# Scores of two attentions on row tiles, negated queries, and sixteen adaLN chunks moved between projections

## The chip, the cores and the metric

The kernel runs on one core of a Trainium2 chip, as one program. The metric is the device time of one execution in microseconds (us). A core has TensorE (PE, matrix products, weight loads shown apart as PEld), VectorE (DVE), ScalarE (ACT), GpSimd (POOL), and SyncE (SP), which here only issues DMAs. Each engine has its own instruction queue; they wait for each other by semaphores.

## The reference

One inference step of a trunk with two layers, on 128 context tokens (group i) and 512 latent tokens (group ii, an 8 x 64 grid) of width 1024, in float32. Each layer, cut to what matters:

```python
shift1, scale1, gate1, shift2, scale2, gate2 = split(silu(c) @ w_ada + b_ada, 6)   # per group
h = rmsnorm(x) * (1 + scale1) + shift1
u_hy, u_na, u_da, u_gate = split(h @ w_in)
y_hy = hyena(u_hy)                      # short conv, two long convolutions by DFT
# NA: 8 heads of 64. context: plain softmax attention over context;
# latent: 8 rows x 16 columns around the query with a relative bias, and 128 cached context keys
s = q @ k.T * 64**-0.5 + bias           # outside the neighbourhood: -1e30
y_na = softmax(s) @ v
# DA: 8 heads, two maps of 32. latent: all 512 latent keys (rotated) and 128 cached keys
p1, p2 = softmax(q1 @ k1.T * 32**-0.5), softmax(q2 @ k2.T * 32**-0.5)
y_da = rmsnorm((p1 - lam * p2) @ v) * subln * (1 - lam_init)
x = x + gate1 * ((sigmoid(u_gate) * lifts of the three y, summed) @ w_out)
x = x + gate2 * swiglu_ffn(rmsnorm(x) * (1 + scale2) + shift2)
```

Outputs are both groups' final rmsnorm and the context keys and values of both attentions.

## The kernel before

Activations stay in SBUF with channels on partitions; the 640 tokens (128 context, 512 latent) are the free dimension. All weights come as 292 strips of 128 x 1024 f32 (512 KB), in a fixed order written out by hand: per layer 12 strips for Hyena (`S_UHY`), 12 for NA (`S_NA`: 4 for queries, 4 for keys, 4 for values), 12 for DA, 36 for gates and lifts, 8 for the output projection and 66 for the FFN. A product is made exact enough by splitting both sides in a rounded high part and a rest, and by three products (`tiles_of`, L446, 48 matmuls a strip; `v_strips`, L467, for values). SP loads a strip (three buffers), POOL writes its high part `whi` (L428) and its low part `wlo` (L430), PE waits for `w_split`. `w_used` rises when PE starts a strip and lets POOL overwrite the high part of the strip before last.

The adaLN modulation of a layer is 48 chunks of 128 outputs; `ada_dot` (L1179) makes one on DVE as two dot products of 128 x 1024 (context and latent), from a 512 KB chunk that ACT's queue loads with `ada_load` (L866), which waits until a buffer is used. In layer 0, chunks 0 to 23 are made at the start, chunks 24 to 39 (`N_ADA1` to `N_ADA2`, 16 chunks, four buffers) between the short convolutions of the Hyena strips (DVE list at L1309 to L1314, ACT's PSUM copies at L974 to L979), the rest in the FFN. ACT waits for the second modulation (`s_modr`) before it loads the first spectrum.

After the Hyena outputs (`s_yhy`), ACT issues loads of the cached NA keys, values and the bias table `rpbr` (L1017 to L1019), then copies the NA projections out of PSUM (L1023). DVE expands the bias table to `bexp` (L1370).

NA runs 40 times (5 query blocks of 128 x 8 heads). Block 0 is the context with 128 keys; blocks 1 and 4 have 3 key blocks, blocks 2 and 3 have 4. Channels hold two heads of 64 per 128 partitions, so DVE masks the queries of a pair to each head's rows (`na_queries`, L1414) and PE multiplies with all 128 rows. Per head: scores, a mask product from bf16 (L645 to L648), on DVE bias and maximum in one (L1388) and its negation `nmx` (L1392), on ACT the exponential with its sum (L1038), on PE the turn of the probabilities (L658), a copy on DVE (L1400), on PE the product with values (L674). PE's list is: scores of head n+1, turn of n, values of n-1.

DA also runs 40 times, with four 32-row groups in 128 partitions (two heads, two maps). DVE masks the queries (`da_queries`, L1464). The two maps use three PSUM banks, with the keys of the two maps in different order:

```python
for n in range(40):
    if n + 2 < 40:
        da_scores(n + 2, True)     # both maps' cache keys, map 1's 512 latent keys
    da_turn(n)
    if n + 2 < 40:
        da_scores(n + 2, False)    # map 2's 512 latent keys
    da_pv(n)
```

DVE reduces each map for its maximum (L1473), negates and scales both (L1475), later forms p1 - lam' p2 in two pieces because of the key order (L1488, L1489); ACT makes both exponentials (L1071, L1073) and copies the turned probabilities `dpt` (L1084); PE turns (L735, L739) and multiplies (L748).

## Time and profile before

| | |
|---|---|
| median of 3 runs | 3244.84 us (3239.64 to 3246.84) |
| the profiled execution | 3243.62 us |
| its span, first to last instruction | 3241.8 us |
| PE busy | 2960.7 us, 91% |
| DVE, ACT, POOL busy | 1506.6, 584.4, 1563.9 us |
| mean granted TensorE clock | 0.946 |

The span is what the profile covers; what lies around it is 1.8 us. A row of a group of instructions has line, engine, operation, tiles as out<-in, shapes and count, then busy time, mean ns of one, and the idle time of its engine just before with the instruction that ended it. PE's records overlap, since matmuls are pipelined: start to start is the time that one costs. An f32 matmul is two records.

### The profile page before, as it was taken

The page shows a single profiled execution, that of the slowest core. Times are in us where ns is not written, and L with a number is a line of the kernel's source. Part 1 is how long each engine was busy: PE and PEld are TensorE (multiplying, and loading weights), DVE is VectorE, ACT ScalarE, POOL GpSimd, SP SyncE. Part 2 cuts the span into 40 slices and gives each one's busy share as a digit, 9 for nine tenths or more (in the row PEclk, how much of TensorE's full clock was granted, in tenths as well). Part 3 has the DMA queues.
Part 4 walks back from the last instruction along what each step waited for, and adds up shares of the span by engine and source line. Part 5 has one row for each costly group of instructions (what it writes and reads, how often), then busy time and mean ns, then how long its engine had stood idle before and what let it go on. Part 6 is the DMA issues. An engine that isn't in the chain of part 4 may idle for free.

```text
span 3241.8 us, 42762 instructions
## 1 busy us (share of the span) xinstructions
PE 2960.7 (91%) x17564; PEld 2614.0 (81%) x17564; DVE 1506.6 (46%) x2553; ACT 584.4 (18%) x1189; POOL 1563.9 (48%) x588
## 2 busy tenths in 40 slices
PE   5898689998979998999998989998979998999997
PEld 1447659895569997999997959896569997999997
DVE  6885871645742214448653572655741124420113
ACT  1123110314520002000102111313520002100100
POOL 1003407061027765778775707061027765777764
PEclk8899799998979998999998999998989998999998
DMA  4434323020002222335432223020002222322222
GB/s 176 136 120 160 91 80 98 4 75 17 1 28 77 75 70 92 110 112 174 147 108 87 72 78 95 11 69 23 1 27 72 79 67 96 99 72 72 79 69 75
DMA packets 76790, 258.86 MB, mean 80 GB/s; under 512 B 9107, under 2 KB 12691, under 8 KB 75060
## 3 DMA queue, kind: packets, MB, share of 16 engines
q1 hardware_dynamic: 49148, 176.96, 17.3%
q10 hardware_dynamic: 27448, 79.17, 7.1%
q8 instruction: 139, 2.28, 0.3%
q14 instruction: 55, 0.45, 0.0%
HBM read 237.75 MB, written 18.35 MB: 79 GB/s over the span
## 4 chain that ended last, share of the span: by engine, by line
PE 77%; DVE 14%; ACT 3%; issue 2%; DMA 2%; DVEq 1%; ACTq 1%; POOLq 0%; POOL 0%
PE PS L446 57%; PE PS L467 3%; PE PS L726 3%; DVE adap L1179 3%; PE PS L530 2%; PE PS L748 2%; PE PS L674 1%; PE PS L735 1%; PE PS L645 1%; PE PS L500 1%; PE PS L613 1%; DVE mx L1473 1%; PE PS L658 1%; PE PS L720 1%; DVE yt L1334 1%
## 5 line engine op out<-in xcount | busy, mean ns | idle before, releaser
L428 POOL TENSOR_SCALAR whi<-wraw 128x1024 fp32r<-128x1024 f32 x292 | 838.2, 2870 | 1606.3 <-PE PS L446 1538.6
L446 PE MATMUL PS<-hhi,whi 128*128 128x320 f32 x3072 | 717.9, 315 | 66.6 <-DVE hlo L1163 43.3
L430 POOL TENSOR_TENSOR wlo<-wraw,whi 128x1024 fp32r<-128x1024 f32 x292 | 725.6, 2485 | 43.0
L446 PE MATMUL PS<-hlo,whi 128*128 128x320 f32 x3072 | 710.5, 313 | 0.0
L446 PE MATMUL PS<-hhi,wlo 128*128 128x320 f32 x3072 | 710.2, 313 | 0.0
L446 PEld LDWEIGHTS PS<-hhi,whi 128*128 128x128 f32 x3072 | 522.2, 192 | 80.9 <-issue 32.5
L446 PEld LDWEIGHTS PS<-hlo,whi 128*128 128x128 f32 x3072 | 523.9, 192 | 0.0
L446 PEld LDWEIGHTS PS<-hhi,wlo 128*128 128x128 f32 x3072 | 523.1, 191 | 0.0
L1179 DVE CUSTOM_DVE_ANT_0 adap<-ada,cond 128x1024 f32<-128x1024 f32 x192 | 338.7, 1764 | 35.0 <-DMA ada<-in_w_ada 12.8
L1562 DVE SCALAR_TENSOR_TENSOR x<-PS,mod,x 128x128 f32<-128x128 f32 x144 | 54.5, 433 | 300.0 <-PE PS L446 300.0
L1595 DVE TENSOR_TENSOR gact<-silu,PS 128x640 f32<-128x640 f32 x44 | 36.1, 821 | 334.8 <-ACT silu L1129 334.8
L446 PE MATMUL PS<-ahi,whi 128*128 128x320 f32 x704 | 163.4, 314 | 13.1 <-DVE alo L1598 13.1
L1473 DVE TENSOR_REDUCE mx<-PS 128x1 f32<-128x640 f32 (+1 forms) x160 | 112.8, 713 | 107.5 <-PE PS L720 53.7
L446 PE MATMUL PS<-alo,whi 128*128 128x320 f32 x704 | 162.6, 313 | 0.0
L446 PE MATMUL PS<-ahi,wlo 128*128 128x320 f32 x704 | 162.4, 312 | 0.0
L1129 ACT ACTIVATE silu<-PS 128x640 f32<-128x640 f32 x44 | 31.1, 706 | 677.0 <-PE PS L446 677.0
L1547 DVE TENSOR_TENSOR sig<-sig,PS 128x640 f32<-128x640 f32 x32 | 26.3, 822 | 271.2 <-PE PS L446 271.2
L726 PE MATMUL PS<-dak,dqz 128*128 128x512 f32 x256 | 134.1, 606 | 0.0
L446 PEld LDWEIGHTS PS<-ahi,whi 128*128 128x128 f32 x704 | 120.0, 191 | 14.2 <-DVE alo L1598 14.2
L748 PEld LDWEIGHTS PS<-dav,dpt 128*128 128x128 f32 x544 | 72.2, 203 | 61.6 <-ACT dpt L1084 60.7
L446 PEld LDWEIGHTS PS<-ahi,wlo 128*128 128x128 f32 x704 | 120.0, 191 | 0.0
L446 PEld LDWEIGHTS PS<-alo,whi 128*128 128x128 f32 x704 | 120.0, 191 | 0.0
(233 smaller groups left out, 4044.8 us busy)
## 6 DMA issues: line engine op xcount, KB each, us to landing
wraw<-in_w_strips SPq DMA_DIRECT2D x292, 512.0 KB, 3.6
ada<-in_w_ada ACTq DMA_DIRECT2D x72, 512.0 KB, 4.5
ada<-in_w_ada SPq DMA_DIRECT2D x24, 512.0 KB, 3.9
spectra<-hst ACTq DMA_DIRECT2D x48, 256.0 KB, 2.0
hld<-spectra ACTq DMA_DIRECT2D x8, 768.0 KB, 5.1
hld<-spectra ACTq DMA_DIRECT2D x12, 512.0 KB, 3.6
cond<-conds ACTq DMA_DIRECT2D x3, 1024.0 KB, 4.8
x<-in_x_in SPq DMA_DIRECT2D x1, 2560.0 KB, 14.7
```

The lines of the kernel that those rows point to most:

```text
L428: nc.gpsimd.tensor_scalar(hi, raw, 1.0, None, ALU.mult)
L430: nc.gpsimd.tensor_tensor(lo, raw, hi, ALU.subtract).then_inc(w_split, 1)
L446: ins = pe.matmul(out[:, h, :], w[:, kt, :], mv[:, h * HALF:(h + 1) * HALF], start=start and m == 0, stop=stop and m == 2)
L467: ins = pe.matmul(PS[:, i, :], hp[:, k, i * 128:(i + 1) * 128], w, start=(k == 0 and m == 0), stop=(k == KD - 1 and m == 2))
L500: pe.matmul(PS[:, 4 + g % 3, :], farg[lay][:, i * 128:(i + 1) * 128], fw3[:, 2 * o + d, :], start=True, stop=True).then_inc(s_hmm, 1)
L530: ins = pe.matmul(out, w, heo[:, i, half, :], start=(r == 0), stop=(r == len(tiles) - 1))
L726: pe.matmul(PS[:, b + 2 * m, :], q[m], dak[:, ch, C:T], start=True, stop=True).then_inc(s_ds, 1)
L748: ins = pe.matmul(PS[:, 7, 128:192], dpt[n % 2][:, i, :], v, start=(r == 0), stop=(r == len(vs) - 1))
L1179: ins = V.tensor_tensor_reduce(adap[s][:, :], ada[s][j][:, :], cond[s][:, c, :], 1.0, 0.0, ALU.mult, ALU.add, mraw[:, 2 * m + c:2 * m + c ...
L1473: V.tensor_reduce(mx[:, q + m:q + m + 1], PSF[:, 512 * b + lo:512 * b + hi], AX, ALU.max)
L1562: ins = V.scalar_tensor_tensor(x[:, m, cols], src, mod[:, gate + m, sgm:sgm + 1], x[:, m, cols], ALU.mult, ALU.add)
L1595: V.tensor_tensor(halves(gact[j % 2][:, :]), halves(silu[j % 2][:, :]), pair(2 * (j % 2) + 1), ALU.mult).then_inc(s_gact, 1)
```

## The change

1. NA scores: `na_scores` now does a pair of heads. The query masking is gone: each head's product uses only its 64 rows of queries and keys. Mask products of both heads come first, then both latent products, then both cache products. Scores have four PSUM banks; turned probabilities and outputs moved to others.
2. The queries are negated (and scaled) when they leave PSUM, the mask and bias are negated, and DVE takes the minimum. That is the bias of the exponential at once (scale -1), so `nmx` and its operation are gone. DA queries are also scaled there.
3. DA scores: map m of a head uses its 32 rows. The latent keys of both maps now have the same order in PSUM (`DA_MAP = 896` columns apart), map 2 in two products of 384 and 128. One reduce covers both maps, one operation forms the difference. Cached keys come from the host with the four groups apart and zeros between (1 MB, was 256 KB), and are multiplied over all 128 rows, after the turn.
4. Layer 0's adaLN chunks 24 to 39 move to the NA projection: their loads stand in ACT's queue behind the NA cache loads and between its PSUM copies, with three buffers (was four); DVE makes them behind the bias expansion and before the first NA head.
5. In layer 0, for strips 13 to 23 (NA, `HI_ON_ACT`), ACT makes the high part, in its queue ahead of the copy of the strip before; POOL makes only the low part.

```diff
-ADA_SLOTS = (2, 4, 4)
+ADA_SLOTS = (2, 3, 4)
+HI_ON_ACT = range(S_NA + 1, S_NA + N_NA)
...
             for n in range(DEPTH * STRIPS):
-                pool.wait_ge(w_in[n % 3], 16 * (n // 3 + 1))
-                if n >= 2:
-                    pool.wait_ge(w_used, n)
-                nc.gpsimd.tensor_scalar(hi, raw, 1.0, None, ALU.mult)
-                pool.drain()
+                if n in HI_ON_ACT:
+                    pool.wait_ge(w_hi, n - HI_ON_ACT.start + 1)
+                else:
+                    pool.wait_ge(w_in[n % 3], 16 * (n // 3 + 1))
+                    if n >= 2:
+                        pool.wait_ge(w_used, n)
+                    nc.gpsimd.tensor_scalar(hi, raw, 1.0, None, ALU.mult)
+                    pool.drain()
                 nc.gpsimd.tensor_tensor(lo, raw, hi, ALU.subtract).then_inc(w_split, 1)
...
+                def na_scores(u):
+                    qb, ch = u // 4, u % 4
+                    heads = [(PS[:, (2 * u + i) % 4, :], slice(64 * i, 64 * i + 64)) for i in range(2)]
+                    if u >= 2:
+                        pe.wait_ge(s_np, nth(lay, s_np, 2 * u - 2))
+                    if qb:
...
+                        for out, r in heads:
+                            pe.matmul(out[:, lat], identb[:, :], maskb[:, MASK0[j]:MASK0[j] + nb, :],
+                                      start=True, stop=False)
+                        for out, r in heads:
+                            pe.matmul(out[:, lat], naq[r, ch, qb * 128:qb * 128 + 128],
+                                      nak[r, ch, C + b0 * 128:C + (b0 + nb) * 128], start=False, stop=True)
+                    for out, r in heads:
+                        pe.matmul(out[:, cache] if qb else out[:, 0:128], naq[r, ch, qb * 128:qb * 128 + 128],
+                                  nckT[r, ch, :] if qb else nak[r, ch, 0:C], start=True, stop=True).then_inc(s_ns, 1)
...
                 for n in range(40):
-                    if n + 1 < 40:
-                        na_scores(n + 1)
+                    if n % 2 == 0 and n + 2 < 40:
+                        na_scores(n // 2 + 1)
...
+                def da_scores(n):
+                    r1, r2 = (slice(64 * (h % 2) + 32 * m, 64 * (h % 2) + 32 * m + 32) for m in range(2))
+                    q1, q2 = (daq[r, ch, qb * 128:qb * 128 + 128] for r in (r1, r2))
...
+                    pe.matmul(PS[:, b, :], q1, dak[r1, ch, C:T], start=True, stop=True)
+                    pe.matmul(PS[:, b + 2, 0:384], q2, dak[r2, ch, C + 128:T], start=True, stop=True)
+                    pe.matmul(PS[:, b + 1, 384:512], q2, dak[r2, ch, C:C + 128], start=True, stop=True)
+                def da_cache_scores(n):
...
+                    k = dckb[:, h // 2, 256 * (h % 2):256 * (h % 2) + 256]
+                    pe.matmul(PS[:, b + 1, 0:128], q, k[:, 0:128], start=True, stop=True)
+                    pe.matmul(PS[:, b + 2, 384:512], q, k[:, 128:256], start=True, stop=True).then_inc(s_ds, 1)
...
                 for n in range(40):
                     if n + 2 < 40:
-                        da_scores(n + 2, True)
+                        da_scores(n + 2)
                     da_turn(n)
                     if n + 2 < 40:
-                        da_scores(n + 2, False)
+                        da_cache_scores(n + 2)
                     da_pv(n)
...
-                if lay == 0:
-                    act.dma_start(cond[1][:, :, :], conds).then_inc(s_cond[0], 16)
-                for k in range(ADA_SLOTS[1] if lay == 0 else 0):
-                    ada_load(1, k, (lay, N_ADA1 + k))
...
-                    if o == 0:
-                        act.wait_ge(s_modr, nth(lay, s_modr, 2))
...
                 act.dma_start(rpbr[:, :, :], a["rpb"][lay]).then_inc(s_ncache, 16)
+                if lay == 0:
+                    act.dma_start(cond[1][:, :, :], conds).then_inc(s_cond[0], 16)
+                    for k in range(ADA_SLOTS[1]):
+                        ada_load(1, k, (lay, N_ADA1 + k))
+                def strip_hi(n):
+                    if n in HI_ON_ACT:
+                        act.wait_ge(w_in[n % 3], 16 * (n // 3 + 1))
+                        act.wait_ge(w_used, n)
+                        A(whi[n % 2][:, :, :], wraw[n % 3][:, :, :], ACT.Copy).then_inc(w_hi, 1)
                 for n in range(8):
+                    strip_hi(lay * STRIPS + S_NA + n + 1)
                     act.wait_ge(s_nq, nth(lay, s_nq, n + 1))
-                    dst, sc = (naq, 0.125) if n < 4 else (nak, 1.0)
+                    dst, sc = (naq, -0.125) if n < 4 else (nak, 1.0)
                     A(halves(dst[:, n % 4, :]), pair((n + 3) % 4), ACT.Copy, scale=sc).then_inc(s_nqe, 1)
+                    for k in range(2 * n + 3, min(2 * n + 5, N_ADA2 - N_ADA1)):
+                        if lay == 0:
+                            ada_load(1, k, (lay, N_ADA1 + k))
...
+                for n in range(8, N_NA):
+                    strip_hi(lay * STRIPS + S_NA + n + 1)
...
-                    for k in range(2 * n, min(2 * n + 2, N_ADA2 - N_ADA1) if lay == 0 else 0):
-                        ada_dot(1, k, N_ADA1 + k)
...
+                if lay == 0:
+                    dve.wait_ge(s_cond[0], 16)
+                    for k in range(N_ADA2 - N_ADA1):
+                        ada_dot(1, k, N_ADA1 + k)
+                    modulation(lay, N_ADA1, N_ADA2)
+                    norm_scale(lay, 1)
...
                 def da_max(n):
...
-                        V.tensor_reduce(mx[:, q + m:q + m + 1], PSF[:, 512 * b + lo:512 * b + hi], AX, ALU.max)
-                    dve.drain()
-                    V.tensor_scalar(nmx[:, q:q + 2], mx[:, q:q + 2], -DA_SCALE, None, ALU.mult).then_inc(s_dm, 1)
...
+                    both = PSF[:, p0:p0 + 2 * DA_MAP].rearrange("p (m n) -> p m n", m=2)
+                    V.tensor_reduce(mx[:, q:q + 2], both[:, :, 0:keys], AX, ALU.min).then_inc(s_dm, 1)
```

The diff is cut: the old forms of the score functions and the two masking functions are left out, as are moved buffers and bank numbers.

## Rows read from the trace of the kernel before

**Rows 1.** Cores view: span and mean granted TensorE clock.
```profile
core 0: 3241.8 us, clock 0.946
```

**Rows 2.** Windows view: window, us, busy PE, PEld, DVE, ACT, POOL, granted clock, DMA share, GB/s.
```profile
281.30:388.90 107.60, 90.59 (x529) 88.53 (x528) 83.70 (x89) 10.02 (x56) 63.12 (x22) 0.87 0.48 158
388.90:483.60 94.70, 74.89 (x272) 49.05 (x272) 73.04 (x132) 14.66 (x31) 0.00 (x0) 0.89 0.20 67
483.60:569.90 86.30, 85.21 (x506) 78.83 (x504) 15.87 (x42) 8.11 (x13) 64.36 (x24) 1.00 0.30 95
745.90:919.10 173.20, 155.08 (x792) 100.13 (x792) 126.36 (x330) 83.99 (x200) 0.00 (x0) 0.92 0.00 1
1788.80:1866.50 77.70, 77.67 (x530) 77.40 (x528) 37.98 (x41) 10.57 (x55) 59.74 (x22) 1.00 0.24 75
1866.50:1949.10 82.60, 70.89 (x273) 46.52 (x273) 62.11 (x113) 13.71 (x26) 0.00 (x0) 0.98 0.23 77
```

**Rows 3.** Chain of waits, 290 to 400 us: start, us, what.
```profile
339.04 1.23 DVE adap L1179
340.39 3.23 DVE adap L1179
```

**Rows 4.** Timeline of PE, layer 0, Hyena strips; start, us.
```profile
334.92 0.90 PE L446 MATMUL PS<-hhi,whi 128*128 128x320 f32 x2 [4.36 <-ACT rawu L979]
```

**Rows 5.** Timeline of ACT in the same strips.
```profile
346.80 0.28 ACT L974 ACTIVATE rawu<-PS 128x128 f32<-128x128 f32 x1 [11.94 <-DVE mraw L1179]
```

**Rows 6.** Timeline of ACT after the Hyena outputs of layer 0.
```profile
494.94 0.34 ACTq L1017 DMA_DIRECT2D nckT<-in_cache_na_k  x1
...
496.36 0.71 ACT L1023 ACTIVATE naq<-PS 128x640 f32<-128x640 f32 x1 [2.38 <-issue]
```

**Rows 7.** Timeline of DVE, same place.
```profile
503.75 3.35 DVE L1370 COPY bexp<-rpbr 128x128 f32<-128x128 f32 x24 [6.70 <-DMA rpbr<-in_rpb]
```

**Rows 8.** DMA issues, 494 to 506 us: count, KB each, us to landing.
```profile
rpbr<-in_rpb ACTq DMA_DIRECT2D x1, 1060.0 KB, 7.9
```

**Rows 9.** DMA issues, 276 to 300 us.
```profile
cond<-conds ACTq DMA_DIRECT2D x1, 1024.0 KB, 9.7
```

**Rows 10.** Timeline of PE in one 4-block NA head.
```profile
618.22 0.86 PE L645 MATMUL PS<-nak,nqz 128*128 128x384 f32 x2
618.92 0.33 PE L647 MATMUL PS<-maskb,identb 128*128 128x384 bf16 x1
619.08 0.38 PE L648 MATMUL PS<-nckT,nqz 128*128 128x128 f32 x2
...
620.58 0.54 PE L645 MATMUL PS<-nak,nqz 128*128 128x384 f32 x1
```

**Rows 11.** Timeline of PE over one DA head and the next.
```profile
804.39 0.66 PE L720 MATMUL PS<-dckT,dqz 128*128 128x128 f32 x4
804.89 1.02 PE L726 MATMUL PS<-dak,dqz 128*128 128x512 f32 x2
805.90 0.66 PE L735 MATMUL PS<-ident,dp 128*128 128x128 f32 x4
...
806.50 1.02 PE L726 MATMUL PS<-dak,dqz 128*128 128x512 f32 x2
807.46 1.10 PE L748 MATMUL PS<-dav,dpt 128*128 128x64 f32 x8
...
808.63 0.66 PE L720 MATMUL PS<-dckT,dqz 128*128 128x128 f32 x4
...
810.74 0.66 PE L735 MATMUL PS<-ident,dp 128*128 128x128 f32 x4 [0.59 <-DVE dp L1489]
```

**Rows 12.** Timeline of ACT in the same DA head.
```profile
806.70 0.70 ACT L1084 ACTIVATE dpt<-PS 128x640 f32<-128x640 f32 x1 [0.61 <-PE PS L739]
```

**Rows 13.** Instruction groups in twenty DA heads: busy us, mean ns, idle before.
```profile
L1473 DVE TENSOR_REDUCE mx<-PS 128x1 f32<-128x640 f32 x40 | 32.8, 820 | 15.8 <-PE PS L726 15.8
...
L1488 DVE SCALAR_TENSOR_TENSOR dp<-dp,coef,dp 128x512 f32<-128x512 f32 x20 | 15.0, 752 | 1.5
```

174 lines of the change are left out of this document (63 added, 111 removed).

## The prediction

> **What bounds the kernel now.** The profile was read in this order: the span, busy time by stage, the chain of waits where two like stages differ, then the timelines of the two attention loops. The profiled execution spans 3241.8 us [rows 1]. The two layers run the same stages, so laying them side by side shows what layer 0 pays extra [rows 2]. From the end of the first Hyena strip to the end of the twelfth, layer 0 takes 107.6 us and layer 1 77.7 us; from there to the first strip of the NA projection, 94.7 and 82.6 us. The reader is to see DVE: 83.7 us busy in layer 0's strips and 38.0 us in layer 1's, while PE is 99.9% busy in layer 1 and 84% in layer 0, and its granted clock is 0.87 there against 1.00. The work that only layer 0 has there is 16 adaLN chunks of two dot products, each 1.23 us alone and 3.2 us where a POOL instruction is in the way [rows 3]. ACT stands in its queue at an adaLN load that waits for a dot (11.94 us), then empties PSUM late, and PE waits for that (4.36 us) [rows 4, 5]. So layer 0's Hyena part is bound by DVE through ACT's queue. The attention loops are different: PE has almost no idle time in them, and what sets a head's time is PE's own list (below).
>
> **The adaLN chunks leave the Hyena projection.** With 32 dots and the loads that block ACT gone, layer 0's stretch should become layer 1's: (107.6 + 94.7) - (77.7 + 82.6) = 42.0 us less. This holds the removed wait of the spectrum load for the second modulation, and the lower clock behind the stalls. Bounds: 30 us if only the strips gain (107.6 - 77.7 = 29.9), 42 if all. I take 42, since nothing else differs between the layers there.
>
> **They arrive in the NA projection.** That stretch has 86.3 us with only 15.9 us of DVE [rows 2], so 32 dots of 1.23 to 3.2 us (39 to 102 us; about 55 with one POOL conflict in four dots) fit in time. The order of ACT's queue does not fit. Strip 13's high part is now made by ACT, behind the wait for the Hyena outputs, three cache loads, the modulation vectors and three adaLN loads. The first cache load issues at 494.94 [rows 6], some 2 us earlier without POOL's strip in the way: 492.7. Three issues take 1.42 us up to the next instruction, seven 3.3 to 4.3 (the last ones move twice as much), so ACT copies from 497.0. A copy of 128x640 takes 0.71 us [rows 6], one of 128x1024 about 1.1 (estimate, 0.71 x 1.6), then POOL's low part about 2.6 us (64.4 / 24 is 2.7 for both kinds): strip 13 is ready at 500.7. Strip 12 begins at 483.6 and takes 7.06 (77.7 / 11), so PE would idle from 490.7, 10 us. Strip 14's copy stands behind the loads of chunks 3 and 4, which wait for dots 0 and 1. DVE can begin these when the rpb table has landed (7.9 us) and 24 copies of 3.35 us together are done, at about 505.5 [rows 7, 8]; the modulation vectors take 9.7 us from issue and are there by about then [rows 9]. Two chunks at 2.6 us end at 510.8, then copy 1.1, low part 2.6 to 3.3 with a conflict: strip 14 starts near 516, where strip 13 would have ended at 507.8 at full clock and about 510.5 after such a gap. For the price of a gap I take the Hyena strips of layer 0: a granted clock of 0.87 over 107.6 us is 28 us at 1.2 in place of 2.4 GHz, and with some five gaps each has 5.6 us of that and loses 2.8 us of work. From strip 15 on, the loads are two strips ahead, POOL has half its work per strip, and PE sets the pace. Sum: 10 + 5 idle and 2 x 2.8 at half clock, about +20 us. Bounds: 12 (both idle times short, no half clock) to 42 (all strips paced as in layer 0's Hyena part, 107.6 / 11 = 9.8 us against 7.06 for 8 strips, on top of the start). The later strips' copies on ACT cost nothing: ACT is busy 8.1 of 86.3 us. If that cover went, PE would wait for a strip. The 1 MB of separated keys is loaded ahead of the twelve strips of the DA projection (12 x 7.06 us) and is hidden by them.
>
> **NA scores on row tiles.** A 4-block head takes 2.36 us (618.22 to 620.58), PE without a gap: latent scores 0.70, mask 0.16, cache scores 0.22, the rest 1.28 [rows 10]. Each f32 matmul is two records, so a head pair has four of about 0.35 and four of about 0.11. Two heads now lie on different 64 rows. If neighbours in the list on different rows run at the same time, the second half of head 0 covers the first of head 1, and the second of head 1 the first cache half: 0.35 x 3 + 0.11 x 3 = 1.4 in place of 1.84, 0.22 us a head. For 3-block heads the same working gives 0.17 (estimate, by the shorter moving side). So 16 x 0.22 + 16 x 0.17 = 6.2 us a layer, 12.5 us in both. If they do not overlap it is nothing, since the negation and the query masking leave DVE, which is not the bound there.
>
> **DA scores on row tiles.** Now a head takes 4.24 us, the next 4.84 (every second head DVE also masks the next queries, and PE waits 0.59): 4.54 on average [rows 11]. PE's list is: cache scores 0.50, first map 1.01, from the transposes to the PV product 1.56, PV 1.17. Afterwards the piece of 1.56 stays, because it is set by ACT's copy of the turned probabilities (806.70 + 0.70, PV at 807.46) [rows 11, 12], although the second map's 0.96 us is taken from under it and only the cache scores' 0.50 is put there. PV stays 1.17. All latent scores now stand together behind PV: two halves of 0.50, two of 0.375, two of 0.125, which is 2.0 us one after the other and 1.62 if the second half of the first map covers the first half of the second. A head: 1.56 + 1.17 + 1.62 = 4.35 us overlapped, 4.70 serial. DVE must fit under this. Its reduce of 640 takes 0.82 us and waited for PE [rows 13]; one over both maps about 1.5 (between 0.82 and 1.64), the joined sum at most 0.94 (0.75 x 640 / 512), small steps and output 0.8: about 3.3 us of work, and the chain transposes 0.65, cache 0.66, reduce 1.5, small steps and sum 1.4 is 4.2. So (4.54 - 4.35) x 32 x 2 = -12.2 us overlapped, (4.70 - 4.54) x 64 = +10 serial. I take overlap, as the tiles touch different rows and PSUM banks, but no row of before shows it.
>
> **Block 0.** Its 8 heads per stage lose the same masking and negation, in short chains that DVE is part of. The nearest row is the 0.59 us that masking cost a pair [rows 11]: 0.3 x 8 heads x 4 stages = -9.6 us. Bounds 0 and double that.
>
> **Going between full and row tiles.** It happens 2 x 20 pairs x 2 layers + 2 x 40 heads x 2 layers = 240 times. Below: nothing, as the change from f32 to bf16 and back around the mask leaves no gap. Above: the tail that a matmul has after its successor has started, 0.66 - 0.50 = 0.16 us [rows 11], 38 us in all. I take nothing. On this the Trainium skill speaks against the change: "TensorEngine Tiling (Array Packing)", Key Properties, says that changing the tiling mode drains the TensorE; by that the time would be up to the 38 us later. No row here has such a switch. "TensorE: Matmul & The Clock Gate", Part 3, says that tiles of different rows run concurrently while matmuls keep their order; by that the overlapped figures hold.
>
> **Sum.** -42 + 20 - 12.5 - 12.2 - 9.6 = -56 us. The profiled execution took 3243.6 us, so 3187; the median of the runs shown is 1.2 us above it: 3188 us.
>
> **Rivals.**
> The tiles run one after the other. For it: f32 halves of one tile share its rows, and the order is kept. Against: different rows. -42 + 20 + 10 - 9.6 = -22, 3223 us.
> Each switch drains. For it: the tail of 0.16 us exists. Against: dense lists show no gap today. -56 + 38 = -18, 3227 us.
> The chunks throttle the NA projection as they did the Hyena one. For it: the same loads in ACT's queue, three buffers. Against: DVE has no conv there. +42 in place of +20, 3210 us.
> Slower: the clock falls to half in the DA loop, because PE's idle moments (1.56 - 0.60 - 0.11 - 0.50, some 0.35 us a head) or the narrow tiles don't hold it up. At half clock PE's list of 4.0 us doubles, so a head takes about 8 us in place of 4.54. It decides from 16 of 64 heads (16 x 3.5 = 56 us); all would cost over 200 us, 3400 us. For it: the stage's clock is 0.92 already. Against: PE is 90% busy there and stays so [rows 2].
> The change does nothing measurable: that the moved dots cost as much as they cost before, with serial tiles.
>
> **Numbers.** Forecast 0.50; serial 0.14; drains 0.12; throttled projection 0.08; better than 3165 0.04; nothing 0.04; half clock or another loss 0.08. The range 3162 to 3228 holds the first four and ends where full drains do. Within 0.2% (6.5 us) is what a measurement of this kernel can't tell from no change: faster 0.88, same 0.04, slower 0.08.
>
> **What would show it.** Right: layer 0's Hyena strips at 7.05 us each; ACT's copy for strip 13 near 497 us less the 42 gained, PE idle some 10 and 5 us before strips 13 and 14 and none later; in DA a head every 4.3 to 4.4 us with the reduce over 1280 elements near 1.5 us; in NA 4-block heads at 2.1 us; in both, PE starts on different rows closer than one record's time. Wrong: heads at 4.7 us and more, gaps at each switch, a clock under 0.9 in either loop, or strips 15 to 20 spaced over 8 us.

## The result and the profile after

The changed kernel takes 3303.52 us (median of 4 runs, 3302.38 to 3306.26) against 3243.12 us for the kernel before in the same comparison: ratio 1.0187, 95% interval 1.017 to 1.0205. It is slower by about 60 us, where 3188 us, some 56 us less than before, was predicted.

The page of the kernel after: busy time of TensorE, and the granted clock in 40 slices.

```profile
PE 3058.2 (93%) x17692; PEld 2739.6 (83%) x17692; DVE 1416.3 (43%) x2169; ACT 594.6 (18%) x1200; POOL 1531.2 (46%) x577
...
PEclk9899989985569998999998999995559998999999
```

PE is busy for 93% of the span, more than the 91% before, and two groups of slices at 5 stand out. They are the differential attention (DA) of the two layers. The mean granted clock has gone from 0.946 to 0.891.

The windows view of the kernel after: first the Hyena stage from the end of strip 0 to the first strip of the neighborhood (NA) projection, that projection, and the NA attention, all of layer 0, then most of the DA attention of layers 0 and 1.

```profile
279.54:438.88 159.34, 149.60 (x802) 124.97 (x801) 100.47 (x154) 24.81 (x87) 59.37 (x22) 0.98 0.27 88
438.88:544.75 105.87, 88.99 (x506) 82.95 (x504) 61.99 (x106) 19.41 (x24) 37.81 (x13) 0.92 0.48 167
544.75:622.79 78.04, 71.88 (x556) 59.48 (x557) 47.26 (x126) 33.93 (x90) 0.00 (x0) 0.91 0.01 5
711.00:925.00 214.00, 208.84 (x822) 167.58 (x815) 99.13 (x191) 80.47 (x194) 0.00 (x0) 0.51 0.00 1
2217.00:2433.00 216.00, 211.73 (x818) 170.19 (x818) 99.16 (x193) 80.99 (x195) 0.00 (x0) 0.50 0.00 1
```

Set beside the kernel before, stage by stage. The NA attention is counted from the last value matmul of its projection to the next projection, the DA attention from its last value matmul to the first turn of its outputs:

| stage | before | after | difference | predicted |
|---|---|---|---|---|
| Hyena stage, layer 0 | 202.3 [rows 2] | 159.3 | -43.0 | -42 |
| NA projection, layer 0 | 86.3 [rows 2] | 105.9 | +19.6 | +20 |
| NA attention, layers 0 and 1 | 87.5 + 87.3 | 78.0 + 78.0 | -18.8 | -12.5 and half of -9.6 |
| DA attention, layers 0 and 1 | 189.9 + 188.6 | 241.6 + 243.6 | +106.7 | -12.2 and half of -9.6 |

The four sum to +64.5 us. The spans differ by 3300.6 - 3241.8 = 58.8; the other 6 us fell away in stretches the change does not touch, none over 2.6 us. So one stage makes the whole result. In it PE is busy 98% of the time, at a granted clock of 0.51 and 0.50, which is the lower level, 1.2 GHz. Before, it stood at half clock only through block 0 and in its last 9 us, and had 0.92 over all [rows 2].

PE's timeline of the kernel after, over one head of the DA loop of layer 0 and the start of the next, at half clock.

```profile
861.37 1.22 PE L720 MATMUL PS<-dak,daq 32*128 32x512 f32 x1
861.38 1.64 PE L721 MATMUL PS<-dak,daq 32*128 32x384 f32 x2
862.39 1.06 PE L720 MATMUL PS<-dak,daq 32*128 32x512 f32 x1
862.82 0.63 PE L722 MATMUL PS<-dak,daq 32*128 32x128 f32 x2
863.38 1.11 PE L741 MATMUL PS<-ident,dp 128*128 128x128 f32 x4
864.29 0.42 PE L745 MATMUL PS<-ident,dp 128*128 128x128 f32 x1
864.50 0.63 PE L731 MATMUL PS<-dckb,daq 128*128 128x128 f32 x2
864.93 0.63 PE L732 MATMUL PS<-dckb,daq 128*128 128x128 f32 x2
865.50 1.97 PE L754 MATMUL PS<-dav,dpt 128*128 128x64 f32 x8
...
867.83 1.22 PE L720 MATMUL PS<-dak,daq 32*128 32x512 f32 x1
```

A head takes 867.83 - 861.37 = 6.46 us, where two took 4.24 and 4.84 before [rows 11]. The tiles do overlap: L720 and L721 start 0.01 us apart, on 32 rows each (the "32x512"), and all latent scores are done in 863.38 - 861.37 = 2.01 us at half clock. There is no gap between the parts, so this is PE's list and nothing else, with each instruction taking twice its time. The clock was at full in layer 0's loop once, from 834.9 to 838.3 us.

PE's timeline of the kernel after, the one head whose scores ran at full clock. From 838.3 us on it is half again.

```profile
836.20 0.69 PE L720 MATMUL PS<-dak,daq 32*128 32x512 f32 x1
836.20 0.91 PE L721 MATMUL PS<-dak,daq 32*128 32x384 f32 x2
836.73 0.59 PE L720 MATMUL PS<-dak,daq 32*128 32x512 f32 x1
836.95 0.38 PE L722 MATMUL PS<-dak,daq 32*128 32x128 f32 x2
837.91 0.78 PE L741 MATMUL PS<-ident,dp 128*128 128x128 f32 x4 [0.57 <-DVE dp L1480]
```

The same scores take 1.13 us to their last end here (836.20 to 837.33), and PE then waits 0.57 us for VectorE's joined sum. So with the clock up the tiles overlap as the prediction meant them to.

### The profile page after: what moved, and what is told of

The parts are those of the page before. It is cut to its first block, busy times and chain, and to the rows that moved or that the text cites. A ratio compares the mean times of both kernels' runs of the same rounds, so it can differ in the third digit from the quotient of the medians.

```text
span 3300.6 us, 42311 instructions
## 1 busy us (share of the span) xinstructions
PE 3058.2 (93%) x17692; PEld 2739.6 (83%) x17692; DVE 1416.3 (43%) x2169; ACT 594.6 (18%) x1200; POOL 1531.2 (46%) x577
## 4 chain that ended last, share of the span: by engine, by line
PE 85%; DVE 9%; ACT 3%; DMA 1%; issue 1%; DVEq 1%; ACTq 1%; POOL 0%
PE PS L445 58%; PE PS L754 5%; PE PS L466 3%; PE PS L529 2%; PE PS L720 2%; PE PS L741 2%; PE PS L673 2%; PE PS L721 1%; PE PS L657 1%; DVE adap L1195 1%; PE PS L499 1%; DMA ada<-in_w_ada 1%; PE PS L596 1%; PE PS L732 1%; PE PS L731 1%
## 5 line engine op out<-in xcount | busy, mean ns | idle before, releaser
L427 POOL TENSOR_SCALAR whi<-wraw 128x1024 fp32r<-128x1024 f32 x281 | 800.4, 2848 | 1555.1 <-PE PS L445 1498.4
L429 POOL TENSOR_TENSOR wlo<-wraw,whi 128x1024 fp32r<-128x1024 f32 x292 | 730.7, 2502 | 186.5 <-ACT whi L1025 145.2
L1467 DVE TENSOR_REDUCE mx<-PS 128x2 f32<-128x1280 f32 (+1 forms) x80 | 102.1, 1278 | 269.7 <-PE PS L732 211.0
L754 PEld LDWEIGHTS PS<-dav,dpt 128*128 128x128 f32 x544 | 121.2, 324 | 26.8 <-ACT dpt L1100 26.8
L754 PE MATMUL PS<-dav,dpt 128*128 128x64 f32 x544 | 135.4, 425 | 7.6 <-ACT dpt L1100 7.6
L720 PE MATMUL PS<-dak,daq 32*128 32x512 f32 x128 | 131.6, 1129 | 0.0
```

The source lines that it names most:

```text
L427: nc.gpsimd.tensor_scalar(hi, raw, 1.0, None, ALU.mult)
L429: nc.gpsimd.tensor_tensor(lo, raw, hi, ALU.subtract).then_inc(w_split, 1)
L720: pe.matmul(PS[:, b, :], q1, dak[r1, ch, C:T], start=True, stop=True)
L754: ins = pe.matmul(PS[:, 7, 128:192], dpt[n % 2][:, i, :], v, start=(r == 0), stop=(r == len(vs) - 1))
L1467: V.tensor_reduce(mx[:, q:q + 2], both[:, :, 0:keys], AX, ALU.min).then_inc(s_dm, 1)
```

## Experiments

Fourteen kernels ran: e1, e2, e7 and e8 four times each, the others once. Four runs of one kernel differ by 9 us at most (e8); the differences between single runs on which the theory of the clock rests are 37 us and more. The first four ask which part costs the time, and whether it is the order of PE's work or the tiles. The theories are named in the expectations: N, that the narrow tiles bring the clock down, and others against it.

**e1: the change with the DA part of before.** The DA loop, its masked queries, its cache keys and its reductions are those of the kernel before; everything else is changed.

```diff
-q1, q2 = (daq[r, ch, qb * 128:qb * 128 + 128] for r in (r1, r2))
+q = [dqz[n // 2 % 2][:, 2 * (n % 2) + m, :] for m in range(2)]
 ...
-pe.matmul(PS[:, b, :], q1, dak[r1, ch, C:T], start=True, stop=True)
+pe.matmul(PS[:, b + 2 * m, :], q[m], dak[:, ch, C:T], start=True, stop=True).then_inc(s_ds, 1)
```

> The changed kernel with the whole DA part of the kernel before (masked queries, two orders of keys, negation); NA tiles and the moved chunks stay. Theory N (the 32-row tiles of DA take the clock down in their own loop): both DA loops go back to a granted clock of about 0.92 and to 190 and 189 us from the last value strip to the first turn of the outputs, so 3300.6 - 51.7 - 55.0 = 3194 us in the profile, about 1.5% faster than before. Rival P (something ahead of the loop, such as the NA tiles, brings the low clock in): the loops stay near 0.5 and the time near 3300 us or above.

Measured: 3197.24 us (3194.89 to 3199.03), ratio to before 0.9859, interval 0.9844 to 0.9873; span 3193.1, clock 0.949. The whole loss lies in the DA part, and the rest of the change is worth 46 us.

**e2: only the chunks move.** The kernel before, with the adaLN chunks in the NA projection and the high parts of its strips made by ScalarE.

```diff
-                if lay == 0:
-                    act.dma_start(cond[1][:, :, :], conds).then_inc(s_cond[0], 16)
 ...
                 for n in range(8):
+                    strip_hi(lay * STRIPS + S_NA + n + 1)
 ...
```

> The kernel before with parts 4 and 5 of the change alone: the sixteen chunks in the NA projection and the high parts on ACT. By the stages of the two traces: -43.0 in the Hyena stage (202.3 to 159.3), +19.8 in the NA projection (86.3 to 106.1): 3243.6 - 23 = 3220 us. If the two interact with the attention loops (another clock, another wait), it is off that by over 5 us.

Measured: 3218.49 us (3217.29 to 3220.23), ratio 0.9923, interval 0.9907 to 0.994. The two terms for the moved chunks, -42 and +20, hold without the rest of the change: together 3243.3 - 3218.5 = 25 us.

**e3: the new order, all rows.** The changed kernel with its list, its single reduction over both maps and its separated cache keys; only the latent and block-0 scores read queries masked by head and map over all 128 rows, as before.

```diff
-r1, r2 = (slice(64 * (h % 2) + 32 * m, 64 * (h % 2) + 32 * m + 32) for m in range(2))
-q1, q2 = (daq[r, ch, qb * 128:qb * 128 + 128] for r in (r1, r2))
+r1 = r2 = slice(0, 128)
+q1, q2 = (dqz[n // 2 % 2][:, 2 * (n % 2) + m, :] for m in range(2))
+pe.wait_ge(s_dqz, nth(lay, s_dqz, n // 2 + 1))
```

> The changed kernel with DA's latent scores from masked queries over all 128 rows, everything else (TensorE's new list, one reduce over both maps, cache scores after the turn) as changed; block 0's scores too. Theory N (narrow tiles): the clock is 1.0 in the steady loop, a head takes 4.7 to 4.9 us (list 1.56 + 1.17 + 2.0), 3205 us in all. Rival L (the new list with its idle moments takes the clock down): clock 0.5, a head about 8.5 us (6.45 seen plus 2.0 of lost overlap), about 3430 us.

Measured: 3196.94 us, span 3195.1, clock 0.949. A head takes 4.58 us, less than the 4.7 to 4.9 expected, but no less than in the kernel before (4.54 and 4.51, table below).

**e4: the tiles, the old order.** The changed kernel with its 32-row tiles, but the cache scores and the first map behind each other and the second map between the turns and the value product, as in the kernel before. So the two maps' tiles are no longer neighbours.

```diff
-                        da_cache_scores(n + 2)
+                        da_second(n + 2)
```

> The changed kernel with the 32-row tiles in the old list: cache scores and map 1 ahead of the turn, map 2 behind it. Theory N: the clock stays at 0.5 and nothing overlaps, a head takes 8 to 8.5 us, 3400 to 3440 us. Rival L: clock 1.0 and 4.3 to 4.6 us a head, 3190 to 3200 us.

Measured: 3438.49 us, span 3435.8, clock 0.875. Half clock throughout, 8.55 us a head. e3 and e4 together: the order alone is harmless, the tiles alone are not, and it isn't that two of them work at once, since in e4 they don't and it is worse.

The windows view over 100 us inside the DA loop of layer 0 of e3, of e4, and of the next two, one fence each. The column to read is the granted clock, the third from the right, beside PE's busy time.

```profile
750.00:850.00 100.00, 91.42 (x549) 69.40 (x548) 68.47 (x120) 50.78 (x109) 0.00 (x0) 1.00 0.00 1
```

```profile
750.00:850.00 100.00, 100.00 (x294) 66.70 (x295) 34.32 (x60) 28.30 (x60) 0.00 (x0) 0.50 0.00 1
```

**e5: 64 rows.** On e3, the scores of both maps read the 64 rows of their head.

```diff
-r1 = r2 = slice(0, 128)
+r1 = r2 = slice(64 * (h % 2), 64 * (h % 2) + 64)
```

> The kernel of e3 (whose list and single reduction are the change's, and whose differential scores read queries masked by head and map over all 128 rows) with one edit: the latent and block-0 scores of both maps read the 64 rows of their head instead of all 128, that is a 64-row tile. Both maps of a head sit in the same 64 rows, so no two of them can overlap. Theory N (it is the 32-row tiles that keep TensorE at half clock; the neighborhood loop on 64-row tiles was granted full clock throughout): the clock stays up and the time is that of e3, 3197 us, within 10. Rival S (any score matmul on fewer than 128 rows does it in this loop, in which TensorE has little idle time): the granted clock is 0.5 in both differential loops, the heads take 6.5 to 7.5 us with nothing to overlap, 3400 to 3450 us. Rival M (in between): the clock changes level within the loop, 3220 to 3380 us.

Measured: 3419.92 us, span 3418.0, clock 0.878; heads of 8.16 us, longer than the 6.5 to 7.5 of rival S, and a time within its range.

```profile
750.00:850.00 100.00, 100.00 (x305) 72.13 (x304) 37.96 (x66) 28.36 (x60) 0.00 (x0) 0.50 0.00 1
```

**e6: one map on its tile.** On e3, the second map on 32 rows, the first on all 128.

```diff
-r1 = r2 = slice(0, 128)
+r1, r2 = slice(0, 128), slice(64 * (h % 2) + 32, 64 * (h % 2) + 64)
```

> The kernel of e3 with one edit: the second map's latent and block-0 scores go back to the 32-row tile with unmasked queries; the first map's stay on all 128 rows. So half as many matmuls run on narrow tiles as in the changed kernel, and none beside another. Theory N with a dose (the clock goes by how much of the loop is narrow): half the dose leaves the clock at full for most of the loop, 3197 to 3260 us. Rival A (one narrow matmul in each head is enough): half clock throughout both loops, heads of about 7 us with no overlap, 3400 to 3440 us, as e4 was. A clock that changes level within the loop gives a time between them.

Measured: 3401.5 us, span 3399.6, clock 0.886. Layer 1 stood at half clock through its blocks 1 to 4, layer 0 from 743.7 to 934.9 us, into its last block. Half the dose is enough, as rival A had it, though a head took 8.28 us in layer 1 and not about 7.

```profile
750.00:850.00 100.00, 100.00 (x306) 69.06 (x305) 37.95 (x66) 28.35 (x60) 0.00 (x0) 0.50 0.00 1
```

Both went against theory N as it stood: it is not 32 rows that matter, 64 do the same. But the NA loop, on 64-row tiles, is granted full clock (1.00 from 565 to 620 us in e3). There the two heads of a pair stand on different 64 rows, side by side.

**e7: NA scores over all rows.** On e3, the NA scores read masked queries over 128 rows too; order and banks stay.

```diff
-heads = [(PS[:, (2 * u + i) % 4, :], slice(64 * i, 64 * i + 64)) for i in range(2)]
+heads = [(PS[:, (2 * u + i) % 4, :], nqz[u % 2][:, i, :]) for i in range(2)]
+pe.wait_ge(s_nqz, nth(lay, s_nqz, u + 1))
```

> The kernel of e3 with the neighborhood scores too on masked queries over all 128 rows: the order of the work, the four banks and the pairs of heads stay as in the change; VectorE masks the queries again, once for each pair. The neighborhood attention took 87.4 us in each layer in the kernel before and 78.0 after the change. Theory T (the gain is that the two heads' tiles work side by side, and that VectorE no longer masks): it is lost again, 85 to 88 us in each layer, 3211 to 3217 us. Rival O (the gain is the order: four banks and scores a whole pair ahead, so that TensorE waits less): the stage stays at 78 to 80 us and the time at 3197 to 3201 us. A mixture would show as a stage between: my estimate is 82 us and 3205 us, since by the rows of before the tiles accounted for 6.2 us of the 9.4 in each layer.

Measured: 3211.5 us (3210.76 to 3212.03), ratio 0.9902, interval 0.9884 to 0.992; span 3209.0. The stage takes 83.3 and 82.3 us in the two layers, against 78.0 and 78.1 in e3 and 87.5 and 87.3 before. The tiles and the masking they spare give 5.2 and 4.2 us; the order, the banks and the spared negation give the rest, 4.2 and 5.0. The whole kernel is 14.6 us slower than e3's one run, which is 5 us more than the two stages; where these lie was not followed.

**e8: ScalarE's queue.** On e3, the copies that make strips 13 and 14 ready go ahead of the transfers, later ones behind the copy of a projection sum, and the loads that wait for VectorE come two strips later.

```diff
                         if o == 1:
+                            if c == 2:
+                                strip_hi(lay * STRIPS + S_NA + 1)
 ...
                 act.wait_ge(s_yhy, nth(lay, s_yhy, 4))
+                strip_hi(lay * STRIPS + S_NA + 2)
                 act.dma_start(nckT[:, :, :], a["cache_na_k"][lay]).then_inc(s_ncache, 16)
 ...
-                    for k in range(2 * n + 3, min(2 * n + 5, N_ADA2 - N_ADA1)):
+                    for k in range(2 * n - 1, 2 * n + 1):
```

> The kernel of e3 with ScalarE's work around the first layer's second projection reordered: the copy that makes the high part of strip 13 is made inside the Hyena output loop, that of strip 14 before the transfers are issued, each later one behind the copy of a projection sum, and the loads of the moved adaLN chunks, which wait for VectorE, are issued two strips later. Theory Q (the 20 us that the projection got longer by are ScalarE's queue: TensorE stood 9.1 us before strip 13 and 7.0 us before strip 14, and both strips ran 2.1 us long at half clock): the projection goes from 106 us back to 86 to 90 us, and the time from 3197 to 3177 to 3182 us. Rival V (VectorE's dots or the transfers of the chunks are the real limit, and come in late at the end instead): the idle time appears before the neighborhood attention, and no more than 5 us are won.

ScalarE's timeline of the kernel after at this place. ACTq is its queue, which issues transfers.

```profile
447.96 0.34 ACTq L1012 DMA_DIRECT2D nckT<-in_cache_na_k  x1
...
449.77 1.89 ACTq L871 DMA_DIRECT2D ada<-in_w_ada  x3
451.76 1.06 ACT L1025 ACTIVATE whi<-wraw 128x1024 fp32r<-128x1024 f32 x1 [4.76 <-issue]
```

The same of e8.

```profile
438.87 1.06 ACT L962 ACTIVATE whi<-wraw 128x1024 fp32r<-128x1024 f32 x1 [1.18 <-PE PS L447]
...
448.56 1.06 ACT L962 ACTIVATE whi<-wraw 128x1024 fp32r<-128x1024 f32 x1 [0.96 <-DVE yhy_lo L1379]
448.56 0.34 ACTq L1025 DMA_DIRECT2D nckT<-in_cache_na_k  x1
```

The first copy is made 12.9 us earlier. Measured: 3186.6 us (3180.97 to 3189.78), ratio 0.9823, interval 0.9807 to 0.9838; span 3179.1, clock 0.953. The projection takes 531.29 - 438.28 = 93.0 us in place of 105.6, and PE's longest waits in it are 3.6 us, for ScalarE's copy of the keys, and 2.5 us, for a strip; they were 9.1 and 7.0, both for strips. So theory Q holds, for 16 us of span and some 10 us of time (the median of four runs against e3's one), where 15 to 20 were expected. This is the fastest version here, ahead of both kernels.

**e9: NA pairs taken apart.** On e3, mask, latents and cache scores of one head, then of the other.

```diff
-                        for out, r in heads:
-                            pe.matmul(out[:, lat], identb[:, :], maskb[...], start=True, stop=False)
-                        for out, r in heads:
-                            pe.matmul(out[:, lat], naq[...], nak[...], start=False, stop=True)
-                    for out, r in heads:
+                    for out, r in heads:
+                        if qb:
+                            pe.matmul(out[:, lat], identb[:, :], maskb[...], start=True, stop=False)
+                            pe.matmul(out[:, lat], naq[...], nak[...], start=False, stop=True)
                         pe.matmul(out[:, cache] ...)
```

> The kernel of e3 with the neighborhood scores written out head by head (mask, latents, cache of one head, then those of the other) and no longer alternating, so that the two heads' 64-row tiles don't stand side by side; the tiles, queries, banks and everything else stay. e5 has shown that 64-row tiles keep the differential loop at half clock, while the same tiles in this loop are granted full clock. Theory O (what counts is how much of the array works: two 64-row tiles side by side are as good as 128 rows, one alone is not): the clock falls in both neighborhood loops, the stage goes from 78 us to 105 to 125 us, the time from 3197 to 3250 to 3290 us. Rival P (the mask products, turns and value products over all 128 rows are enough in this loop, side by side or not): the clock stays, the stage takes 82 to 86 us, since the overlap is lost as in e7, 3205 to 3213 us.

Measured: 3363.13 us, span 3361.3, clock 0.907. The windows view of e9: the whole NA stage of layer 0, and 55 us in its middle.

```profile
545.25:702.22 156.97, 152.02 (x558) 119.17 (x557) 47.96 (x126) 34.05 (x90) 0.00 (x0) 0.51 0.01 2
565.00:620.00 55.00, 55.00 (x197) 42.53 (x196) 17.80 (x46) 9.95 (x26) 0.00 (x0) 0.50 0.00 1
```

PE's timeline over latent scores: the two heads' in the kernel after, with the order of e3 and at full clock, and one head's in e9, at half. From the first start to the start of the next matmul it is 0.74 us (to 594.14) for two heads and 1.44 us (to 592.83) for one.

```profile
593.40 0.92 PE L644 MATMUL PS<-nak,naq 64*128 64x384 f32 x4
```

```profile
591.39 1.65 PE L646 MATMUL PS<-nak,naq 64*128 64x384 f32 x2
```

The stage doubles, from 78 to 157 us, more than the 105 to 125 expected, because PE never gets its clock back in it. Not one matmul, tile, bank or reader is other than in e3: only the order in PE's list. This fits theory O: what counts is how much of the array is at work while TensorE is busy, and two 64-row tiles side by side count as 128 rows. One rival is left: PE's list now goes twice as often from full rows to tiles and back. e13 and e12 below answer it.

**e10 and e11: redundant work beside the 32-row tiles.** On the changed kernel, one more matmul in each head of blocks 1 to 4, whose result nobody reads; e10 on the other head's 64 rows, e11 on all 128.

```diff
+rf = slice(64 * (1 - h % 2), 64 * (1 - h % 2) + 64)   # e11: slice(0, 128)
 pe.matmul(PS[:, b, :], q1, dak[r1, ch, C:T], start=True, stop=True)
+pe.matmul(PS[:, b + 1, 0:384], daq[rf, ch, qb * 128:qb * 128 + 128], dak[rf, ch, C:C + 384], start=True, stop=True)
```

> The changed kernel (32-row tiles in the differential loops) with one redundant matmul added to each head of blocks 1 to 4: behind the first map's latent scores, the other head's 64 rows of the same chunk times 384 keys, on their own 64-row tile beside the two 32-row tiles, into the columns between the maps that nobody reads (those of the cache scores are overwritten afterwards). Nothing that is used changes. Theory O (the clock goes by how much of the array works): four groups of rows now work where two did, and the clock comes back to full for most of both loops: the heads then take 4.4 to 4.9 us and the time is 3190 to 3230 us, in spite of the added work. Rival A (a narrow matmul in the loop is enough, whatever stands beside it): half clock as before, 3303 us plus up to 64 times the part of the added 1.5 us that doesn't overlap, 3303 to 3400 us.

> The changed kernel with one redundant matmul of 384 keys over all 128 rows added to each head of blocks 1 to 4, in the same place and with the same unread output as in e10; it can't overlap with the narrow tiles, so all of it is added to TensorE's list (0.75 us at full clock, 1.5 us at half). Theory O: full-row work raises the share of the array that works and the clock returns to full: heads of 5.1 to 5.4 us, 3220 to 3250 us. Rival A: half clock, heads of 7.9 us, 3400 us. If e10 comes back to full clock and this one doesn't, it is the overlap and not the sum of the work that counts.

Measured: 3530.46 and 3535.7 us, clocks 0.867 and 0.864, 10.02 and 10.03 us a head. Neither theory had such a time. PE's timeline of e10 over the scores of one head shows why.

```profile
849.14 1.06 PE L721 MATMUL PS<-dak,daq 32*128 32x512 f32 x1
850.13 1.65 PE L722 MATMUL PS<-dak,daq 64*128 64x384 f32 x2
851.70 1.64 PE L724 MATMUL PS<-dak,daq 32*128 32x384 f32 x2
853.14 0.63 PE L725 MATMUL PS<-dak,daq 32*128 32x128 f32 x2
```

The 64-row tile starts when the first map's 32-row tile is done, and the second map's when the 64-row tile is done, though all lie on different rows and banks. Tiles of two heights don't work side by side. (The Trainium skill, "TensorEngine Tiling (Array Packing)", Key Properties, says that changing the mode drains TensorE; this trace agrees in so far as the overlap is gone, and it shows no idle time at the change. What a change costs is read from e13, in the part on the prediction.) So the fill, in e11 as in e10, took the two narrow tiles apart and made the narrow share larger, and these two runs decide nothing between O and A. They called for a fill of the same height.

**e12, e13, e14: fills of the same height.** In blocks 1 to 4 of all three the second map's last 128 keys go over all rows. e14 is e3 with both maps' other latent scores on 32-row tiles; e12 adds a third 32-row tile beside them; e13 is e5 with a tile on the other 64 rows beside each of its 64-row tiles.

```diff
 # e14, and with the last line e12
+pe.matmul(PS[:, b, :], daq[r1, ch, cols], dak[r1, ch, C:T], start=True, stop=True)
+pe.matmul(PS[:, b + 2, 0:384], daq[r2, ch, cols], dak[r2, ch, C + 128:T], start=True, stop=True)
+pe.matmul(PS[:, b + 1, 0:384], daq[rf, ch, cols], dak[rf, ch, C:C + 384], start=True, stop=True)
 ...
 # e13, behind each of the two 64-row matmuls of e5
+pe.matmul(PS[:, b + 1, 0:384], daq[rf, ch, qb * 128:qb * 128 + 128], dak[rf, ch, C:C + 384], start=True, stop=True)
```

> The kernel of e3, with its blocks 1 to 4 changed: the latent scores of both maps (512 and 384 keys) on the 32-row tiles of the change, the second map's other 128 keys over all 128 rows with masked queries, and a third 32-row tile beside the two, the other head's first map times 384 keys, which writes columns that nobody reads or that the cache scores overwrite. All three have the same height and a bank each, so that they can work side by side. Theory O (what counts is how many rows of the array work while TensorE is busy: the fill of e10 had another height, stood in a row with the tiles and so took them apart): three groups of rows instead of two work in a third of the time. If that is enough, the clock comes back to full and the time is 3180 to 3205 us; if it isn't, it stays at half as in e14. Rival A (a narrow matmul in a loop with TensorE always busy is enough): half clock, 3290 to 3320 us, the fill costing nothing beside the others.

> The kernel of e5 (64-row tiles one after the other, half clock, 3420 us) with a fill of the same height: beside each map's latent scores the other head's 64 rows times 384 keys, again into columns that nobody uses; the second map's last 128 keys go over all 128 rows with masked queries. So 128 rows work through the latent scores, as in e3, but in two tiles. Theory O: full clock in both loops as in e3, heads of 4.4 to 4.7 us, 3190 to 3215 us. Rival A (any matmul on a narrow tile): half clock in both loops, heads of 7.5 to 8 us, 3400 to 3430 us. The two can hardly be confused.

> The kernel of e12 without the fill: two 32-row tiles side by side for 512 and 384 keys, all else over 128 rows. Both theories expect the half clock of the changed kernel in both loops, heads of 6.4 to 6.6 us and 3295 to 3320 us. If the clock holds instead (3180 to 3200 us), then it was the quarter of the second map's keys on a narrow tile by itself that made the difference, and only e13 says anything of the fill.

Measured: e12 3219.15 us (clock 0.936), e13 3218.63 us (0.949), e14 3256.29 us (0.919). PE's timeline of e13 from the last value products of a head over the latent scores of another to the next turns: L724 and L727 are the real 64-row tiles, L725 and L728 the fills, L730 the last 128 keys.

```profile
822.03 0.39 PE L762 MATMUL PS<-dcv,dpt 128*128 128x64 f32 x2
822.35 0.69 PE L724 MATMUL PS<-dak,dqz 64*128 64x512 f32 x1
822.35 0.91 PE L725 MATMUL PS<-dak,daq 64*128 64x384 f32 x2
822.88 0.59 PE L724 MATMUL PS<-dak,dqz 64*128 64x512 f32 x1
823.10 0.48 PE L728 MATMUL PS<-dak,daq 64*128 64x384 f32 x1
823.31 0.48 PE L727 MATMUL PS<-dak,dqz 64*128 64x384 f32 x1
...
823.63 0.48 PE L727 MATMUL PS<-dak,dqz 64*128 64x384 f32 x1
824.04 0.49 PE L730 MATMUL PS<-dak,dqz 128*128 128x128 f32 x2
824.37 0.60 PE L749 MATMUL PS<-ident,dp 128*128 128x128 f32 x4
```

The windows view of e13 over 100 us of each layer's loop, then that of e12, then of e14.

```profile
750.00:850.00 100.00, 92.65 (x605) 71.60 (x604) 65.95 (x117) 49.61 (x105) 0.00 (x0) 1.00 0.00 1
2240.00:2340.00 100.00, 92.72 (x607) 71.87 (x606) 66.12 (x115) 49.61 (x105) 0.00 (x0) 1.00 0.00 1
```

```profile
750.00:850.00 100.00, 95.30 (x486) 69.61 (x486) 56.83 (x99) 42.21 (x90) 0.00 (x0) 0.71 0.00 1
2240.00:2340.00 100.00, 88.00 (x613) 63.65 (x612) 70.99 (x124) 53.26 (x113) 0.00 (x0) 1.00 0.00 1
```

```profile
750.00:850.00 100.00, 96.31 (x428) 70.61 (x428) 53.38 (x93) 39.97 (x84) 0.00 (x0) 0.67 0.00 1
2240.00:2340.00 100.00, 94.88 (x453) 69.61 (x452) 56.99 (x101) 42.73 (x91) 0.00 (x0) 0.72 0.00 1
```

e13 is the largest step: work that nobody needs, put on the idle 64 rows beside e5's tiles, makes the kernel 3419.9 - 3218.6 = 201 us faster, because the clock is full again. It differs from e5 in two things, the fill and the last 128 keys over all rows. The last keys count too, since with them alone on all rows (e14) the clock is 0.71 where the changed kernel has 0.51. The cleanest pair is e12 and e14, which differ by the third tile alone: 3256.3 - 3219.2 = 37 us. In both pairs PE's list goes from full rows to tiles and back once a head with the fill and without it, so the number of changes is not what the clock follows. All DA runs in one table, blocks 1 to 4, by the latent scores of a head. Clock and head are means from VectorE's joined sum of the tenth head to that of the thirty-ninth, since the fortieth has no scores behind it:

| | rows at work in the latent scores | layer 0: clock, us a head | layer 1: clock, us a head |
|---|---|---|---|
| before | 128 | 1.00, 4.54 | 1.00, 4.51 |
| e3 | 128 | 1.00, 4.58 | 1.00, 4.58 |
| e13 | 64 + 64 side by side, 128 for the last keys | 1.00, 4.79 | 1.00, 4.80 |
| e12 | 32 + 32 + 32 side by side, 128 for the last keys | 0.79, 5.21 | 0.98, 4.52 |
| e14 | 32 + 32 side by side, 128 for the last keys | 0.71, 5.65 | 0.73, 5.52 |
| after | 32 + 32 side by side, 32 for the last keys | 0.51, 6.40 | 0.50, 6.45 |
| e6 | 128, then 32 | 0.57, 7.56 | 0.50, 8.28 |
| e5 | 64 | 0.50, 8.16 | 0.50, 8.17 |
| e4 | 32 | 0.50, 8.55 | 0.50, 8.55 |
| e10 | 32, then 64, then 32 | 0.50, 10.02 | 0.50, 10.02 |
| e11 | 32, then 128, then 32 | 0.50, 10.03 | 0.50, 10.03 |

Both theories expected the half clock of the changed kernel for e14; it came out between. e12 and e13 are some 14 and 4 us above theory O's ranges, e12 because layer 0 got its clock back late, and far below rival A's. So the clock isn't lost by any narrow tile, and it comes back step by step as more rows work at a time.

## Why the prediction was wrong

**The step that failed** is the clock. The prediction named it as its slower rival, that "the clock falls to half in the DA loop", gave as a possible reason that "the narrow tiles don't hold it up", and set it at 0.08, on the ground that "PE is 90% busy there and stays so". PE was 98% busy, and the clock fell all the same: busy time was taken as what the clock follows, and e9, e12 and e13 show that it isn't enough: how many rows work side by side counts too. With the DA term replaced by what it measured (+106.7 in place of -17.0, block 0's share with it), the prediction's own sum gives 3188 + 123.7 = 3312 us, against 3303.5 measured.

**The rival's size** was too high: "a head takes about 8 us" and 3400 us, against 6.46 us and 3303.5. It doubled PE's serial list of 4.0 us, but the tiles overlap at half clock as at full, which saves on the scores: 2.01 us at half clock is 1.0 us of work at full. Where the tiles stand one after the other, in e4, the head takes 8.55 us and the kernel 3438 us, and the rival's price is about right. So the measured time lies outside the range of 3162 to 3228 and short of the rival's.

**The DA loop at full clock** was forecast at 4.35 us a head. The changed kernel had no whole head so, and what it would take is not shown. The new order by itself gains nothing: 4.58 us a head in e3, and 190.3 and 190.0 us for the stages, which took 189.9 and 188.6 before. The tiles are what could have gained. The overlap was real and larger than forecast, 1.13 us for the latent scores in place of 1.62. The nearest rows are the last heads of e12, at full clock and with no more queries to mask, three in a row of 4.14 us in layer 0. So 4.35 was not too low, and with the clock up some (4.54 - 4.14) x 64 = 26 us were to be had in both layers; that is an estimate, as e12's last keys go over all rows. It stands against the 107 us that the clock took.

**The chunks leave the Hyena stage**: -42 predicted, -43.0 measured. **They arrive in the NA projection**: +20 predicted, +19.6 measured, at the two places forecast, 9.1 us before strip 13 and 7.0 before strip 14 (10 and 5 predicted). e2 confirms both together (25 us), and e8 that it is ScalarE's queue.

**NA on tiles**: -12.5 and -4.8 for its block 0 predicted, -18.8 measured. The mechanism holds, since without the tiles (e7) 5.2 and 4.2 us are lost, but half the gain comes from the four banks, the pair of heads ahead and the spared negation, of which the prediction had priced only the last, and only in block 0. That the sum came so near is in part luck.

**Switching** between full and narrow tiles was taken at nothing, as the dense lists of before have no gap. There is no gap here either, but the starts lie further apart. PE's timeline of e3, which has no tiles in this loop, at the same places as e13's above:

```profile
803.82 0.39 PE L757 MATMUL PS<-dcv,dpt 128*128 128x64 f32 x2
804.04 1.08 PE L723 MATMUL PS<-dak,dqz 128*128 128x512 f32 x2
...
805.60 0.38 PE L725 MATMUL PS<-dak,dqz 128*128 128x128 f32 x2
805.82 0.60 PE L744 MATMUL PS<-ident,dp 128*128 128x128 f32 x4
```

The two value passes ahead of the scores take 0.22 us from start to start, and 0.32 in e13 ahead of its tiles. The second of L727's passes takes 0.41 us ahead of full rows, the first 0.32. The two full-row passes for the last keys take 0.33 us behind the tiles in e13, and 0.22 in e3. So going in and out costs some 0.3 us a head at full clock, which is what the rival in which each switch drains charged (two of 0.16). This term was mis-sized too. It is hidden in the NA loop by an overlap larger than forecast: the latent scores of a pair take 0.74 us (593.40 to 594.14), where 1.05 was forecast. Tiles of two heights follow each other only in e10, where the overlap is lost.

Open: how the clock follows the rows, beyond the order in the table. In every DA run the clock was at half in block 0, and what the tiles decide first is whether it comes back: in layer 0 at 730.7 us in e3, at 735.3 in e13, at 807.1 in e12, at 817.0 in e14, and never within the loop in e4 and e5. That it also falls again from full is shown at 838.3 us in the changed kernel, at 743.7 in e6 and at 854.5 in e14. e12's two layers differ (0.79 and 0.98) with the same code; in what phase the loop comes out of block 0 may matter, and no run tested it. That e11's full-row fill did not help was not taken further: it also took the tiles apart.

## What to carry to other kernels

Before scores or other short contractions go onto row tiles, fill the rows: as many tiles of one height side by side as make 128, or zeros in the idle rows of a masked operand, which add nothing to a matmul; they need VectorE to mask, and PE waited 0.59 us a pair for that [rows 11]. In a loop in which TensorE sets the pace, the 1 us in 4.5 that overlap can take off the scores is worth less than the clock, so read the granted clock of the stage first, and treat a matmul on fewer rows as one that may halve it. And when work is moved to a stage with time to spare, look at the order of the queue it enters: here the moved loads cost 20 us, and 13 of them came back by putting two copies ahead of them and the waiting loads two strips later.

## What the runs showed of the hardware

- The granted clock of a TensorE that is 97 to 100% busy stayed at its lower level, 1.2 GHz, for 120 to 370 us at a stretch, in loops where part of the matmuls had only 32 or 64 of the 128 rows at work (after, e4, e5, e6, e9, e10, e11). The Trainium skill, "TensorE: Matmul & The Clock Gate", Part 1, has the clock follow how busy TensorE has been; here it does not follow busy time alone. Rows that hold zeros count as at work: the masked queries of e3 are zero in 96 of their 128 rows, the keys pass over all of them, and its loop ran at 1.00.
- The order of the same matmuls decides it: NA pairs alternating, 78 us; head by head, 157 us (e9).
- Tiles of one height on different rows start within 0.01 us of each other, two (861.37 and 861.38) or three of them (829.78, 829.78 and 829.79 in e12); tiles of different heights waited for one another (e10).
- Going from full rows to tiles and back cost some 0.3 us a round at full clock, with no idle time in the trace (e13 against e3).
- A 32-row matmul of 512 keys takes no less time than one over 128 rows: 0.53 us from start to start of its two passes at full clock in the changed kernel (836.20 to 836.73), 0.50 before [rows 11].
